# First products of three norms issued by feature tile between the transposes, and an early dummy root

## The reference

```
def second_block(x, mem, ...):
    h = rms_norm_2(x, norm_mix_g)
    x = x + hybrid_mixer(h, w_in, ...)          # h @ w_in: glu gate, glu value, q, k, v, gates
    h = rms_norm_2(x, norm_x_g)
    x = x + cross_attention(h, mem, wq, ...)    # h @ wq
    h = rms_norm_2(x, norm_ffn_g)
    x = x + swiglu(h, w_in, w_out)              # a, b = split(h @ w_in)
...
def rms_norm_2(x, g):
    y = x * rsqrt(mean(x * x, axis=-1) + EPS)
    return y * g
```

## Time and profile before

| | us |
|---|---|
| median of 3 runs | 2166.68 (2165.76 to 2171.54) |
| profiled execution, its own time | 2168.2 |
| its span in the trace | 2166.4 |
| TensorE busy | 1903.8 (88%) |
| VectorE busy | 658.9 (30%) |
| ScalarE busy | 583.5 (27%) |
| GpSimd busy | 630.1 (29%) |

### The profile page before, as it was taken

How to read it: one execution, slowest core, us unless ns; L and a number is a source line. 1 busy time by engine, 2 the same in 40 slices (tenths; PEclk the granted TensorE clock), 3 DMA queues, 4 the chain that set the end, 5 groups by cost and what they waited for, 6 DMA issues and landing times.

```text
span 2166.4 us, 21286 instructions
## 1 busy us (share of the span) xinstructions
PE 1903.8 (88%) x8472; PEld 1229.9 (57%) x8472; DVE 658.9 (30%) x1369; ACT 583.5 (27%) x1042; POOL 630.1 (29%) x361
## 2 busy tenths in 40 slices
PE   4999989498878788749999999888899889999997
PEld 2544337233222222238888878544687568888886
DVE  6551265511001001145897024465111211000001
ACT  3113462100000000042241243566143423222211
POOL 0002233400000000044432324555354324555542
PEclk8999999699899999969997998999999999999999
DMA  9453201889999999853232412000233122232221
GB/s 374 155 228 121 103 1 64 338 349 425 430 427 427 430 428 428 345 181 108 87 105 52 122 54 97 20 21 21 98 117 117 39 81 76 87 104 91 91 104 58
DMA packets 94306, 379.22 MB, mean 175 GB/s; under 512 B 6235, under 2 KB 35291, under 8 KB 79884
## 3 DMA queue, kind: packets, MB, share of 16 engines
q1 hardware_dynamic: 88048, 356.47, 42.3%
q0 software_dynamic: 3456, 12.58, 1.5%
q10 hardware_dynamic: 2716, 8.98, 1.0%
HBM read 357.50 MB, written 20.51 MB: 174 GB/s over the span
## 4 chain that ended last, share of the span: by engine, by line
PE 69%; DMA 17%; DVE 6%; ACT 4%; issue 2%; POOL 1%; SPq 0%; DVEq 0%; ACTq 0%; POOLq 0%
DMA slots<-in_w_expert_up 14%; PE bank L717 14%; PE bank L718 14%; PE bank L719 14%; PE bank L692 11%; PE bank L1029 7%; PE bank L1227 2%; PE bank L1207 1%; PE bank L845 1%; ACT area L1727 1%; POOL low_r L2439 1%; DMA slots<-in_w_ada 1%; PE bank L763 1%; PE bank L1050 1%; PE bank L772 1%
## 5 line engine op out<-in xcount | busy, mean ns | idle before, releaser
L2439 POOL TENSOR_TENSOR low_r<-slots,high_r 128x2048 fp32r<-128x2048 f32 x87 | 400.5, 4604 | 604.6 <-ACT high_r L1411 604.6
L718 PE MATMUL bank<-xl_r,high_r 128*128 128x512 f32 (+1 forms) x864 | 331.2, 383 | 0.0
L717 PE MATMUL bank<-area_r,high_r 128*128 128x512 f32 x800 | 315.1, 394 | 0.9 <-POOL low_r L2439 0.9
L1029 PE MATMUL bank<-slots,area 128*64 128x512 f32 x992 | 250.5, 664 | 72.4 <-DMA slots<-in_w_expert_up 38.9
L719 PE MATMUL bank<-area_r,low_r 128*128 128x512 f32 x800 | 313.0, 391 | 0.0
L1411 ACT ACTIVATE high_r<-slots 128x2048 fp32r<-128x2048 f32 x87 | 166.3, 1913 | 439.1 <-PE bank L719 411.6
L1029 PEld LDWEIGHTS bank<-slots,area 128*64 128x64 f32 x992 | 77.4, 152 | 244.8 <-issue 154.0
L718 PEld LDWEIGHTS bank<-xl_r,high_r 128*128 128x128 f32 x864 | 163.9, 190 | 32.0 <-issue 0.5
L717 PEld LDWEIGHTS bank<-area_r,high_r 128*128 128x128 f32 x800 | 151.5, 189 | 33.2 <-POOL low_r L2439 1.2
L719 PEld LDWEIGHTS bank<-area_r,low_r 128*128 128x128 f32 x800 | 151.4, 189 | 31.4
L2265 DVE SCALAR_TENSOR_TENSOR bank<-area,cols,bank 128x512 f32<-128x512 f32 x232 | 153.5, 756 | 0.0
(11 more groups left out here) (378 smaller groups left out, 2696.6 us busy)
## 6 DMA issues: line engine op xcount, KB each, us to landing
slots<-in_w_expert_up SPq DMA_DIRECT2D x32, 2048.0 KB, 18.8
slots<-in_w_expert_down SPq DMA_DIRECT2D x32, 2048.0 KB, 19.8
slots<-in_w_expert_gate SPq DMA_DIRECT2D x30, 2048.0 KB, 18.3
slots<-in_w_in SPq DMA_DIRECT2D x15, 2048.0 KB, 8.8
slots<-in_w_ada SPq DMA_DIRECT2D x11, 2048.0 KB, 12.2
slots<-in_ffn_in_w SPq DMA_DIRECT2D x22, 1024.0 KB, 6.6
slots<-in_ffn_out_w SPq DMA_DIRECT2D x5, 2048.0 KB, 7.8
slots<-in_w_out SPq DMA_DIRECT2D x4, 2048.0 KB, 8.4
```

What stands on the lines that cost most here:

```text
L717: nc.tensor.matmul(out, xh, yh, start=start and n == 0, stop=False)
L718: nc.tensor.matmul(out, xh, yl, start=False, stop=False)
L1029: last = nc.tensor.matmul(banks[which][piece, :], XT[b][:, k, piece], w[side][:, k, :], start=k == 0, stop=k == KT - 1)
L2439: nc.gpsimd.tensor_tensor(low_half(m), raw_half(m), high_half(m), ALU.subtract).then_inc(s["w_low"], 1)
```

## The change

At all three norms TensorE's order changes. Ahead of the transposes of feature tile c (c = 4 to 7) it now waits until tile c - 4 has left its bank in both parts and issues the products of feature tile c - 4: at "mix" and "normx" 12 matmuls (four output tiles), which together make the first half of glu_g0 and xq; at "ffn" 6 matmuls (output tiles 0 and 1 of ffin), and the products of k = 4 to 7 for these two follow behind the transposes. The number of matmuls and transposes is the same. Where both halves' products went by output tile before, the first half (at "ffn" the first two output tiles) goes by feature tile. On ACT one root of a constant column into an unused column of `small` is added ahead of the norm of "ffn".

```diff
+            def first_half_by_feature_tile(stage):
+                held = {}
+                def product(k):
+                    if k == 0:
+                        held["w"] = parts(FIRST_HALF[stage], 4)
+                        held["out"] = [bank_of(FIRST[stage] + t) for t in range(4)]
+                    wh, wl = held["w"]
+                    for t in range(4):
+                        c = slice(t * P, (t + 1) * P)
+                        last = split_product(held["out"][t][:, :], [(wh[:, k, c], wl[:, k, c], hTS[0][:, k, :],
+                                                                     hTS[1][:, k, :])], start=k == 0, stop=False)
+                    if k == 3:
+                        last.then_inc(s["half_used"], 1)
+                return product
...
+            def feature_tile_split(stage, c):
+                n = XP[stage] + c
+                pe.wait_ge(tiles_emptied[split_bank(n)], (n - XP["mix"]) // N_TILE_BANKS + 1)
...
-            def split_norm_transposes(stage, XN):
+            def split_norm_transposes(stage, XN, product):
                 pe.wait_ge(s["xn_ready"], TT * (NORM_NO[stage] + 1))
                 for c in range(KT):
+                    if c >= N_TILE_BANKS:
+                        feature_tile_split(stage, c - N_TILE_BANKS)
+                        product(c - N_TILE_BANKS)
                     split_transposes(XP[stage] + c, [(t * P, XN[:, t, c * P:(c + 1) * P]) for t in range(TT)])
...
-            split_norm_transposes("mix", XN4)
+            split_norm_transposes("mix", XN4, first_half_by_feature_tile("glu_g0"))
             for n in range(2):
-                split_feature_major(f"glu_g{n}", hTS, later_columns=None if n else "mix")
+                split_feature_major(f"glu_g{n}", hTS, later_columns=None if n else "mix", halves=(0, 1) if n else (1,))
...
-            split_norm_transposes("normx", XN4)
+            split_norm_transposes("normx", XN4, first_half_by_feature_tile("xq"))
             for n in range(2):
-                split_feature_major("xq", hTS, n, later_columns=None if n else "normx")
+                split_feature_major("xq", hTS, n, later_columns=None if n else "normx", halves=(0, 1) if n else (1,))
...
-            split_norm_transposes("ffn", XN4)
+            def first_pair():
+                held = {}
+                def product(k):
+                    if k == 0:
+                        held["w"] = parts(FIRST_HALF["ffin"], KT)
+                        held["out"] = [bank_of(FIRST["ffin"] + n) for n in range(2)]
+                    wh, wl = held["w"]
+                    for n in range(2):
+                        c = slice(n * P, n * P + P)
+                        last = split_product(held["out"][n][:, :], [(wh[:, k, c], wl[:, k, c], hTS[0][:, k, :],
+                                                                     hTS[1][:, k, :])], start=k == 0, stop=k == KT - 1)
+                        if k == KT - 1:
+                            last.then_inc(s["proj_done"], 1)
+                return product
+            product = first_pair()
+            split_norm_transposes("ffn", XN4, product)
+            for k in range(KT - N_TILE_BANKS, KT):
+                feature_tile_split("ffn", k)
+                product(k)
             for j in range(FT // 2):
-                for n in range(4):
+                for n in range(0 if j else 2, 4):
...
             split_weights(FIRST_HALF["ffin"] + 1)
+            nc.scalar.activation(small[:, 156:157], small[:, 152:153], ACT.Sqrt)
             norm(XN4, s["dve_emptied"], emptied("dve", FIRST["xo"] + 4))
```

More of the change, by code:

```diff
@@ L725, in parts, with split_groups @@
                 return (high_half(m).rearrange("p (k n) -> p k n", k=k), low_half(m).rearrange("p (k n) -> p k n", k=k))
-            def split_groups(stage, n, tiles, width, operands, more_tiles=0, later_columns=None):
-                for half in range(2):
+            def split_groups(stage, n, tiles, width, operands, more_tiles=0, later_columns=None, halves=(0, 1)):
+                for half in halves:
                     m = FIRST_HALF[stage] + 2 * n + half
@@ L749, in split_token_major, with split_feature_major @@
                                                        wh[:, kw, :], wl[:, kw, :]), more_tiles)
-            def split_feature_major(stage, x, n=0, tokens=S, later_columns=None):
+            def split_feature_major(stage, x, n=0, tokens=S, later_columns=None, halves=(0, 1)):
                 split_groups(stage, n, 4, tokens,
@@ L754, in split_feature_major @@
                                                        x[0][:, k, 0:tokens], x[1][:, k, 0:tokens]),
-                             later_columns=later_columns)
+                             later_columns=later_columns, halves=halves)
+            def first_half_by_feature_tile(stage):
[12 more added lines that the diff above has]
+                return product
             def transposes(n, pieces):
@@ L1317, in _ @@
                     for half in range(2):
-                        if j == n == 0 and half:
-                            split_emptied("ffn")
                         last = split_product(bank[:, :], [(wh[:, k, c], wl[:, k, c], hTS[0][:, k, :], hTS[1][:, k, :])
```

## The result

The changed kernel takes 2175.23 us (median of 6 runs, 2174.32 to 2183.56) where the kernel before takes 2166.47 (6 runs, 2165.08 to 2171.54): a ratio of 1.0047, 95% interval 1.0033 to 1.0061. It is 8.8 us slower. The profiled execution took 2179.65 us with a span of 2177.8.

The account below looks back on a forecast made before the run. TensorE, busy 69% of the span, was taken to bound the kernel. Terms 8.1 + 2.3 (mix) + 1.3 (normx) + 1.4 (ffn) = 13.1 us over the 2166.68 median gave 2179.8 us, range 2173 to 2186.

Parts of the forecast that it names:

- Mix, the late split: At mix, glu_g0's second weight split queues behind ACT's copy of tile 7, so the second half starts 8.1 us later.
- compounding rival: Clock stays low through mix's product(0), +1.7 us; short stops at normx and ffn lower it, 1.6 each; 2184.7 us, chance 0.12.
- Mix, the clock behind the stop: At mix, TensorE's 7.5 us gap brings the half clock back for the products behind it, +2.3 us.
- Normx: At normx, the first-bank wait comes back as a 1.8 us wait for tile 7; second half starts 1.3 us later.
- the lower bound: At normx, if the clock doesn't fall, 0.3 us are gained instead.
- Ffn: At ffn, ffin's second weight split comes late and the third product group starts 1.4 us later, the root's gain included.
- The root: At the ffn norm, the early dummy root takes the table load off the path, -1.08 us.
- counting waits: TensorE's six waits from 958 to 1370 us, 6.2 us together, taken to mean a first-norm delay moves everything behind.
- Absorbed: Rival: the late weight split at mix and ffn is absorbed or isn't late; sum +2.8 us, 2169.5 us, chance 0.11.
- the clock pays: Rival: products between transposes hold or lift the clock at all three norms; 7.4 us gained, 2159.3 us, chance 0.03.

Follow-up runs that it names:

- mix_warm: The change at the mix norm alone, plus 64 extra transposes during TensorE's stop; 2178.96 us against 2167.32 before.
- after_early: The changed kernel with the second weight splits of glu_g0 and ffin moved ahead of ScalarE's copies; 2175.09 us against 2167.43 before.
- mix_only: The kernel before with the change at the mix norm alone; 2174.49 us against 2167.50 before.
- before_early: The kernel before with only the second weight splits of glu_g0 and ffin moved ahead of ScalarE's copies; 2170.88 us against 2167.43 before.
- normx_only: The kernel before with the change at the normx norm alone; 2171.92 us against 2167.50 before.
- root_xq: The kernel before with the early root and xq's second weight split behind ScalarE's copies at normx, old product order; 2161.49 us against 2167.32 before.

## Why the prediction was right

**Mix, the late split.** Right in mechanism and place. 8.1 us were forecast and 9.53 came: the 1.4 more are product(0), which ran at the low clock nearly throughout. I had that as a part of the compounding rival at 1.7, and it is the term that was mis-sized. It isn't a matter of one execution: the clock rose 8.9 to 9.1 us after the first transpose in the five new-order kernels with the 0.8 us stop ahead of product(0), 6.1 in mix_warm, which lacks the stop, and 3.3 to 6.0 in the eight with the old order. The other half of that rival (short stops at normx and ffn bringing the clock down) didn't happen after either stop, of 1.65 and 1.74 us.

**Mix, the clock behind the stop.** 2.3 forecast, 3.0 measured (6.2 us at half rate), and mix_warm's profile takes them away; its median doesn't show it.

**Normx.** 1.3 forecast, -0.07 measured: the clock didn't fall, which I had as the lower bound (-0.3). That bound set a new order without the fall against an old one with it. At an equal clock the order costs 1.4 us where it stays up (18.74 against 17.38) and 1.5 where it falls (20.34 in after_early against 18.81), so the 1.3 was right for the order and the measured -0.07 owes the rest to the clock. That the wait isn't saved but added to was right (1.65 forecast as 1.8). Its cause I had not looked for: ACT's own split ahead of the copies, worth 1.8 us when moved.

**Ffn.** The root gave 1.08 us, as forecast. The stage as a whole was forecast at +1.4 and measured +1.38, with a wait on POOL of 1.74 where I had 2.2.

**The sum.** The stages add to 12.55 - 0.07 + 1.38 = 13.9 us in the profile, 13.1 forecast. The medians say 8.8. The difference lies in the clock between the stages: from q2 to normx the changed kernel made up 6.2 us in its profile (12.55 at q2, 6.39 at normx's first transpose) in stages it doesn't touch, where mix_only made up 2.7. Counted matmul by matmul, it made up 0.8 us at the gates' products of 48 columns, 0.8 in the products right behind them, 1.3 behind the compression's, 0.4 at the compressed scores and 2.9 at the end of the attention. All are places where the clock changed its level: between these two points it was at half for 54.6 us before and for 41.0 after, and 13.6 us at 0.47 is 6.4. The waits in this stretch are the same in both profiles to 0.3 us each. I had ruled out that anything later could give time back, by counting waits, and that step was wrong: no wait gave it back, the level of the clock did. How much of it is luck of an execution and how much holds on average isn't settled; the medians put it at some 5 us. The forecast of 2179.8 was 4.6 too high, inside its range for reasons that partly offset: +1.4 and +0.7 at mix, -1.4 at normx, some -5 between the stages. That the single number came as near as it did is in part luck.

**The rivals.** "Absorbed" and "the clock pays" are out: mix_only has the full loss, and the products between the transposes didn't lift the clock earlier (964.0, 9.1 us after the first transpose, against 5.9 before); with the stop ahead of product(0) it rose later. What the change was to fill, idle time of TensorE between the transposes, was there at one norm of three, and there it had another cause.

## What to carry to other kernels

Before work is put between two steps of a chain, look at what each in-order engine has queued behind the last step: here one instruction of 1.9 us on ScalarE, which nobody moved, fed 4.6 us on GpSimd that had been hidden by the very products that were moved. Work put on one engine should be checked against the others for what it runs beside, since a subtraction on GpSimd beside a scaling on VectorE cost more (4.2 us) than the wait it was to remove. And ask of every idle time what ended it before filling it: 1.8 of the 2.1 us at normx were had by exchanging two lines.

## What the runs showed of the hardware

A VectorE scaling of 128x1024 from SBUF to SBUF (0.75 us) didn't finish while GpSimd's tensor_tensor of 128x2048 ran; whichever began first made the other wait. In the fourteen profiles four scalings took 6.97 to 7.11 us eight times in place of 2.74 (three of the eight at normx, in before_early, normx_only and root_xq, where TensorE had other work). Each time the subtraction had begun 1.63 to 1.98 us after the first scaling; where it began 2.07 to 2.38 us after, it was the subtraction that took longer (4.77 to 5.07 us). Transposes of 128x128 fp32 kept TensorE's granted clock at 1.00 through a stretch of 7.15 us, and the clock's levels between the same two points moved the time by up to 6.2 us from one profile to another, with no wait in the trace to show for it.
